# Encoder layer with an S5 mixer: the start of the S5 stage, the order of its loop and its hand-over to the output projection rearranged

## The reference

```python
lam_dt  = (lam_re + i*lam_im) * exp(log_step)
b_bar   = (exp(lam_dt) - 1) / lam * b
h[t]    = exp(lam_dt) * h[t-1] + b_bar @ u[t]            # one direction; the other runs over flipped tokens
y       = gelu(y_fw + y_bw + d * u)
out     = (y * sigmoid(y @ w_glu + b_glu)) @ w_out
h       = layer_norm(ALPHA * x + out)
```

## Time and profile before

| what | value |
|---|---|
| median of 3 runs | 2645.22 us |
| the profiled execution's own time | 2644.07 us |
| its span, first to last instruction | 2642.3 us |
| mean granted TensorE clock | 0.973 |
| PE busy / DVE busy / POOL busy over the span | 94% / 73% / 28% |

### The profile page before, as it was taken

How to read it: one execution, slowest core, us unless ns; L and a number is a source line. 1 busy time by engine, 2 the same in 40 slices (tenths; PEclk the granted TensorE clock), 3 DMA queues, 4 the chain that set the end, 5 groups by cost and what they waited for, 6 DMA issues and landing times. The chain is left out here.

```text
span 2642.3 us, 39850 instructions
## 1 busy us (share of the span) xinstructions
PE 2488.7 (94%) x12860; PEld 2085.5 (79%) x12860; DVE 1920.4 (73%) x3122; ACT 900.0 (34%) x1455; POOL 727.2 (28%) x557
## 2 busy tenths in 40 slices
PE   7678799999999999999999999998799999999997
PEld 6567687878888878887888888887677888887886
DVE  8879826777877758884667666676586777785887
ACT  3223324243333335523322223223124333333641
POOL 6768810243333310001111111112024333331000
PEclk9888899999999999999999999999899999999999
DMA  4143314056677678722010110100404667667863
GB/s 146 56 118 105 97 56 160 13 150 214 192 222 214 204 264 281 233 102 63 25 41 24 40 32 24 40 24 16 159 8 135 203 207 220 209 200 259 296 207 130
DMA packets 442288, 355.97 MB, mean 135 GB/s; under 512 B 30272, under 2 KB 376512, under 8 KB 438464
## 3 DMA queue, kind: packets, MB, share of 16 engines
q1 hardware_dynamic: 442176, 354.52, 42.9%
HBM read 296.31 MB, written 58.13 MB: 134 GB/s over the span
## 5 line engine op out<-in xcount | busy, mean ns | idle before, releaser
L2514 PE MATMUL ps<-aT_hi,w_hi 128*128 128x512 f32 x624 | 250.7, 402 | 3.8 <-DVE hg_q_raw L2793 2.0
L2464 POOL TENSOR_TENSOR w_lo<-w_raw_plain,w_hi 128x1024 fp32r<-128x1024 f32 x38 | 90.9, 2401 | 575.3 <-ACT w_hi L62 575.3
L2514 PE MATMUL ps<-aT_hi,w_lo 128*128 128x512 f32 x624 | 245.2, 393 | 0.0
L2514 PE MATMUL ps<-aT_lo,w_hi 128*128 128x512 f32 x624 | 243.8, 391 | 0.0
L616 PE MATMUL ps<-aT_hi,hgo_w_sets 128*128 128x512 f32 x640 | 203.0, 393 | 0.0
L616 PE MATMUL ps<-aT_hi,s5o_w_sets 128*128 128x512 f32 x640 | 202.7, 393 | 0.0
L1284 POOL TENSOR_TENSOR s5o_w_sets_plain<-s5o_w_sets_plain 128x512 f32<-128x512 f32 x80 | 109.9, 1374 | 216.7 <-DMA s5o_w_sets_plain<-in_ffn_w_in_dram 216.7
L1284 POOL TENSOR_TENSOR hgo_w_sets_plain<-hgo_w_sets_plain 128x512 f32<-128x512 f32 x80 | 110.6, 1383 | 212.8 <-DMA hgo_w_sets_plain<-in_ffn_w_in_dram 212.8
L616 PEld LDWEIGHTS ps<-aT_hi,hgo_w_sets 128*128 128x128 f32 x640 | 120.4, 188 | 26.4
L616 PEld LDWEIGHTS ps<-aT_hi,s5o_w_sets 128*128 128x128 f32 x640 | 120.2, 188 | 26.3
L2514 PEld LDWEIGHTS ps<-aT_hi,w_hi 128*128 128x128 f32 x624 | 117.5, 188 | 26.9 <-DVE hg_q_raw L2793 2.4
(11 more groups left out here) (445 smaller groups left out, 6246.9 us busy)
## 6 DMA issues: line engine op xcount, KB each, us to landing
s5o_w_sets_plain<-in_ffn_w_in_dram SPq DMA_DIRECT2D x168, 256.0 KB, 3.2
hgo_w_sets_plain<-in_ffn_w_in_dram SPq DMA_DIRECT2D x168, 256.0 KB, 3.3
w_raw_plain<-in_hg_w_in_dram SPq DMA_DIRECT2D x40, 512.0 KB, 3.9
aT_hi_plain<-in_ffn_w_out_dram SPq DMA_DIRECT2D x64, 256.0 KB, 4.6
s5o_w_sets_plain<-in_ffn_w_in_dram SPq DMA_DIRECT2D x96, 128.0 KB, 2.7
hgo_w_sets_plain<-in_ffn_w_in_dram SPq DMA_DIRECT2D x96, 128.0 KB, 2.8
s5o_hidden<-s5o_home_plain SPq DMA_DIRECT2D x11, 1024.0 KB, 7.0
hgo_hidden<-hgo_home_plain SPq DMA_DIRECT2D x11, 1024.0 KB, 6.8
```

The lines of the kernel that those rows point to most:

```text
L2464: g.tensor_tensor(w_lo[b][:, :, :], w_raw[b][:, :, :], w_hi[b][:, :, :].bitcast(F32), ALU.subtract).then_inc(E[f"w_lo_done{b}"], 1)
L2514: ins = t.matmul(ps[:, half, :], w[b][:, kk, :], x[:, kk, cols], start=(kk == 0 and q == 0), stop=(kk == KT - 1 and q == 2))
```

## The change

- **Front.** The tables on DVE shrink to `tables_to_inverse`; eight operations go to POOL (`first_power`). DVE makes both halves of `bl(0)`; POOL waits until the scan factors (`mu`) are done before it splits w_in slice 1 and makes `bl(1)`. `cl(0)` forward moves from POOL to DVE, behind `scan(0)`, and from POOL's front goes one `make_cl`. `inputs(2)` is cut in two, around `start_state(1)`; on ACT `place_c(0)`, a half of `keep_u(2)` and `keep_state(0)` come ahead of `place_c(1)`.
- **Loop.** For n = 2 to 5 the first half of `inputs(n+2)` stays ahead of `turn_bl(n+1)` and the second half goes behind it. On ACT the second `keep_u(n+2)` and `split_w(n+3)` go behind `place_b`, `keep_min`, `place_c`. `turned_diagonal(n)` moves to just after the first level of `scan(n)`. POOL's and SP's order in the loop stay.
- **Hand-over.** Inside the S5 block ACT and DVE split the first piece of w_out ahead of the gates of slice 6 and the first four rows of x ahead of those of slice 7; PE's last gate slice runs row by row over both halves. The next block's PE starts on these without a wait. Some buffers are laid out anew for that (`UNDER_FIRST_WEIGHTS`, `s5_gap`, `k.first` and `k.hi0` allocated in the S5 block).

The core of the diff, in the order of the file (the next block first, then the S5 block by SP, PE, ACT, DVE, POOL):

```diff
-        k.first, k.hi0, k.lo0 = (k.sb("w_" + n, [P, PIECE], F32R, keep=True) for n in ("raw0", "hi0", "lo0"))
+        k.lo0 = k.sb("w_lo0", [P, PIECE], F32R, keep=True)
...
-            s.wait_ge(S["w_lo"], KT)
+            s.wait_ge(S["w_lo"], KT - PIECE_DONE)
             load_rows(gamma_mid, beta_mid)
-            s.wait_ge(S["x_lo"], KT)
+            s.wait_ge(S["x_lo"], KT - ROWS_DONE)
             for half in range(2):
                 tiles = slice(4 * half, 4 * half + 4)
                 s.dma_start(h[:, tiles, :], residual_v[:, tiles, :]).then_inc(S[f"back{half}"], 16)
-            s.wait_ge(S["w_lo"], 2 * KT)
+            s.wait_ge(S["w_lo"], 2 * KT - PIECE_DONE)
...
-                        t.wait_ge(S["x_lo"], at + 1)
-                        t.wait_ge(S["w_lo"], 4 * n + at + 1)
+                        if at >= ROWS_DONE:
+                            t.wait_ge(S["x_lo"], at + 1 - ROWS_DONE)
+                        if n or not PIECE_DONE:
+                            t.wait_ge(S["w_lo"], 4 * n + at + 1 - PIECE_DONE)
                         for tt in range(4):
                             project(n, at, tt, 2 * tt + dh)
                 else:
-                    t.wait_ge(S["x_lo"], KT)
-                    t.wait_ge(S["w_lo"], 4 * n + 4)
+                    t.wait_ge(S["x_lo"], KT - ROWS_DONE)
+                    t.wait_ge(S["w_lo"], 4 * n + 4 - PIECE_DONE)
...
-                    if not natural or n and at == 3:
+                    if (4 * n + at == KT - 1) if natural else (4 * n + at >= ROWS_DONE):
                         split_x(4 * n + at)
-                    if n or not natural:
+                    if n:
...
-                    split_x(4 * n + at)
-                    split_piece(n, at)
+                    if 4 * n + at >= ROWS_DONE:
+                        split_x(4 * n + at)
+                    if n or not PIECE_DONE:
+                        split_piece(n, at)
...
+            s.wait_ge(S["next_lo"], FIRST_ROWS + 4)
...
-                    t.wait_ge(S["bl"], (n + 1) * BL - BL // 2)
+                    t.wait_ge(S["bl"], (n + 1) * BL)
                 if n == 0:
                     t.wait_ge(S["c_kept"], 8)
                 elif n == 1:
                     t.wait_ge(S["min_kept"], 4)
                 else:
                     t.wait_ge(S["kern_rows_done"], n)
-                    t.wait_ge(S["cl_fw"], (n - 1) * CLF)
+                    t.wait_ge(S["cl_fw"], n * CLF)
                 for m in range(4):
                     if n == 0:
-                        t.wait_ge(S["bl" if m < 2 else "bl_bw"], BL // 4 * (m % 2 + 1))
+                        t.wait_ge(S["bl"], BL // 4 * (m + 1))
...
-                t.wait_ge(S["cl"], (n + 2) * CLS)
-                t.wait_ge(S["cl_fw"], (n or 1) * CLF if n < KT - 1 else (n - 1) * CLF + CLS)
+                t.wait_ge(S["cl"], (n + 1) * CLS)
+                t.wait_ge(S["cl_fw"], ((n or 1) + 1) * CLF if n < KT - 1 else n * CLF + CLS)
...
             turn_bl(1)
-            inputs(2, (0, 1))
+            inputs(2, (0,))
             start_state(1)
+            inputs(2, (1,))
             make_kern(0)
...
                 across_chunks(n - 1)
                 if 2 <= n < KT - 2:
-                    inputs(n + 2, (0, 1))
+                    inputs(n + 2, (0,))
                 if n < KT - 1:
                     turn_bl(n + 1)
+                if 2 <= n < KT - 2:
+                    inputs(n + 2, (1,))
 
...
                     if kks[-1] == KT - 1:
                         ins.then_inc(S["unit"], 1)
+                    elif n == KT - 1 and half == 1:
+                        ins.then_inc(S["row_free"], 1)
...
                 t.wait_ge(S[f"glu_lo{n % 2}"], n // 2 + 1)
-                for half in range(2):
-                    t.wait_ge(S["gated"], 2 * (n - 4) + half + 1)
-                    gate_part(n, (half,), range(KT))
+                if n < KT - 1:
+                    for half in range(2):
+                        t.wait_ge(S["gated"], 2 * (n - 4) + half + 1)
+                        gate_part(n, (half,), range(KT))
+                else:
+                    t.wait_ge(S["gated"], 2 * (n - 4) + 2)
+                    for kk in range(KT):
+                        gate_part(n, (0, 1), (kk,))
...
-                a.wait_ge(S["min_kept"], 4 * (n + 1))
+                a.wait_ge(S["min_kept"], 4 * ((n or 1) + 1))
+                if n == 1:
+                    a.wait_ge(S["cl_fw"], CLF)
...
             keep_min(1)
+            place_c(0)
+            keep_u(2, (0,))
+            keep_state(0)
             place_c(1)
-            keep_u(2)
+            keep_u(2, (1,))
             split_w(3)
-            keep_state(0)
             keep_kern_rows(0)
             place_b(1)
             for n in range(1, KT):
                 keep_kern_rows(n)
                 if n >= 2:
                     keep_y(n - 1)
-                if n + 2 < KT:
+                if n == 1:
                     keep_u(n + 2)
-                if n + 3 < KT:
                     split_w(n + 3)
+                if n >= 2 and n + 2 < KT:
+                    keep_u(n + 2, (0,))
                 if n == KT - 2:
                     split_glu(0)
                 if n + 1 < KT:
...
                         place_c(n + 1)
                 if n == 1:
                     keep_y(0)
+                if n >= 2 and n + 2 < KT:
+                    keep_u(n + 2, (1,))
+                    if n + 3 < KT:
+                        split_w(n + 3)
...
             for n in range(KT):
+                if n == KT - 2:
+                    a.wait_ge(S["early"], 16)
+                    a.wait_ge(S["out_done"], KT)
+                    for at in range(4):
+                        split_hi(a, in_four(k.first)[:, at, :], in_four(k.early)[:, at, :]).then_inc(S["next_w_hi"], 1)
+                if n == KT - 1:
+                    for kk in range(FIRST_ROWS):
+                        a.wait_ge(S["row_free"], kk + 1)
+                        a.wait_ge(S["mixed"], 2 * (kk + 1))
+                        split_hi(a, in_tokens(k.aT_hi[:, kk, :]), in_chunks(row(kk))).then_inc(S["next_x_hi"], 1)
                 gates(n)
...
-            def tables_to_first_power():
-                v.wait_ge(S["tab_act"], 4)
-                done(v.tensor_tensor(W["c1"], W["half"], W["half"], ALU.mult))
-                done(v.tensor_scalar(W["c1"], W["c1"], -2.0, None, ALU.mult))
-                done(v.tensor_scalar(W["cos"], W["c1"], 1.0, None, ALU.add))
+            def tables_to_inverse():
+                v.wait_ge(S["tab_act"], 2)
                 done(v.tensor_scalar(W["t"], W["tanh"], -1.0, 1.0, ALU.mult, ALU.add))
                 done(v.reciprocal(W["t"], W["t"]))
-                done(v.scalar_tensor_tensor(W["em"], W["tanh"], 2.0, W["t"], ALU.mult, ALU.mult))
-                done(v.tensor_scalar(W["e"], W["em"], 1.0, None, ALU.add))
                 done(v.memset(asc[:, 0, :, 0], 1.0))
                 done(v.memset(asc[:, 1, :, 0], 0.0))
-                done(v.tensor_tensor(asc[:, 0, :, 1], W["e"], W["cos"], ALU.mult))
-                done(v.tensor_tensor(asc[:, 1, :, 1], W["e"], W["sin"], ALU.mult))
-                assert link.n == FIRST_POWER
+                assert link.n == INVERSE
 
             def tables_to_input_factors():
+                v.wait_ge(S["exp"], EXP)
...
-                if n == KT - 1:
+                if n == 1:
+                    turned_diagonal(0)
+                if n >= 2:
                     turned_diagonal(n)
                 for lv in range(1, LV):
                     last = whole(lv, False, last)
-                if n == 1:
-                    turned_diagonal(0)
-                if 2 <= n < KT - 1:
-                    turned_diagonal(n)
...
-            tables_to_first_power()
+            tables_to_inverse()
             for n in range(4, XT):
                 split_x(n)
             tables_to_input_factors()
             v.wait_ge(S["b_kept"], 4)
             make_b_bar(v, 0)
             v.wait_ge(S["pow"], POW)
-            make_bl(v, 0, (0,))
+            make_bl(v, 0)
             scan_factors()
             v.wait_ge(S["c_turned"], 4)
             v.memset(state[:, :, :, 0], 0.0).then_inc(S["pads"], 1)
             scan(0)
+            v.wait_ge(S["c_placed"], 1)
+            make_cl_in_psum(v, 0)
             for n in range(1, KT):
                 if n < KT - 1:
-                    v.wait_ge(S["c_placed"], n)
+                    v.wait_ge(S["c_placed"], n + 1)
...
             for n in range(KT):
+                if n == KT - 2:
+                    for at in range(4):
+                        v.wait_ge(S["next_w_hi"], at + 1)
+                        v.tensor_tensor(in_four(k.hi0)[:, at, :], in_four(k.early)[:, at, :],
+                                        in_four(k.first)[:, at, :].bitcast(F32), ALU.subtract).then_inc(S["next_lo"], 1)
+                if n == KT - 1:
+                    for kk in range(FIRST_ROWS):
```

(48 more changed lines are left out.)

36 lines of the change are left out of this document (24 added, 12 removed).

## The result

Over the runs of both kernels the changed one took 2652.3 us (median of 8), the kernel before 2644.8 (median of 8): ratio 1.0026, 95% interval 1.0015 to 1.0037. That is 7.5 us slower, on the side and near the size of the forecast (2653.8). The profiled execution of the changed kernel took 2650.0 us, its span 2648.2 us, at a mean granted clock of 0.974.

The account below looks back on a forecast made before the run. PE was taken as the bound over the span, with a loop through ACT's and POOL's splits pacing the S5 stage. Terms -0.4 + 11.3 - 2.3 = plus 8.6 us gave 2652.7 profiled, 2653.8 as median; range 2641 to 2667.

Parts of the forecast that it names:

- front: Start of the S5 stage up to the end of `inputs(4)`: forecast at 165.1 us against 165.52, minus 0.4 us.
- loop: Two periods from `inputs(4)` to `inputs(6)`, forecast at 37.1 us each against 31.67 and 31.22: plus 11.3 us.
- hand-over: Passage from S5 to the next block: PE forecast to start at 411.0 instead of 413.25, minus 2.3 us.
- the border: The hand-over to the next block, forecast at minus 2.3 us, bounds minus 5.3 to nothing.
- the turns between the halves: 16 turns put ahead of the input product's second half: 3.0 us taken, between 2.2 and 3.69.
- DVE's stall at the diagonal: In the loop `turned_diagonal(n)` waits for kernel rows that need POOL's `make_cl`: 6 us, costed at nothing.
- the scan factors: 26 short DVE operations in the front, forecast at 5.5 us instead of 23.0, ending at 46.7.
- all steps from there to the end of `inputs(4)` are the same: Front, from step 2's turns, forecast 3.4 us sooner: nothing changes but the turns now in the middle, 3.0 us.
- DVE sets the pace: Faster rival: with w_in's split in time, the loop is DVE's 30.2 us and the time 2634; chance 0.12.
- the zero: The end of `inputs(n+2)`, from which the forecast counts times in a loop period.
- The forecast's chain for the kernel before: Loop: end of `inputs(n+2)`, ACT's copy and split, POOL's split, `make_cl`, PE's kernel, output products, next `inputs`; 31.67 and 31.22 us.
- The clock rival: Slower rival: the product's second half runs at half pace, 4.6 us in each of two periods: 2663; chance 0.13.

Follow-up runs that it names:

- the old order: Changed kernel with both halves of the input product ahead of the turns again: 0.9983 of the kernel before; with the border undone too: 0.9993.
- the diagonal's experiment: Changed kernel with DVE's turned diagonal back at its old place behind the scan's upward levels: 1.0028 of the kernel before.
- moving POOL's split: Changed kernel with POOL's split of the weights behind the six instructions of `make_cl` in the loop: 0.9943 of the kernel before.

## Why the prediction was right, step by step

The forecast's sum was -0.4 (front), +11.3 (loop), -2.3 (hand-over). The three parts by themselves, as differences of ratios times 2644.8: the loop 1.0026 - 0.9983 = 0.0043, plus 11.4 us; the border 1.0026 - 1.0039 = -0.0013, minus 3.4 us (by the old order, 0.9983 - 0.9993, minus 2.6); the front 0.9993 - 1, minus 1.9 us, with nothing inside its interval. Each of them has an interval of 3 to 4 us around it, so by the times only the loop's sign is shown; the border's rests on PE's wait in the traces, and the front's is open. The experiments also cut the change in another way than the forecast: the 3.0 us of the turns inside `inputs(4)`, which the forecast has in its front, belong to the loop order. By that cut it forecast -3.4 for the front, +14.3 for the order and -2.3 for the border.

In the traces, cut as the forecast is, the front came at +2.4, the loop at +10.2 and the hand-over at -3.4, in all 9.2 at the next block's first product. That the sum is so near 8.6 owes something to luck: the front was forecast 2.8 us too low, the other two 1.1 too high each, and a scatter of several us lies behind them.

**Loop: right in mechanism and nearly in size.** The period was forecast at 37.1 us and came at 36.6; PE's waits were named at 2.4 us ahead of the turns (0.4 to 1.3 came) and about 5 ahead of the kernel (4.1 to 5.8 came). The term that was off is the turns between the halves, 3.0 us: the halves came 196.42 to 198.72 apart, 2.3, near the lower bound of 2.2. DVE's stall at the diagonal was put at 6 us and took 2.3 to 4.5, as the scan's first level took 5.4 us (172.21 to 177.57) where 3 were charged, and costing it at nothing is what the diagonal's experiment bears out.

**Front: right at the scan factors, wrong behind them.** 5.5 us for the factors was exact, the x split gained 2.1 and not 3.1 us, `bl(0)` started 1.0 us later than forecast, and that 1.0 and 0.2 more stand at the third turns (123.72, forecast 122.5). The step that failed is "all steps from there to the end of `inputs(4)` are the same". The turns themselves were not the same (stretch, length, busy and count of PE, PEld, DVE, ACT, POOL, granted clock; the changed kernel, then the kernel before):

```profile
123.70:127.60 3.90, 3.83 (x16) 3.06 (x16) 0.00 (x0) 1.80 (x4) 3.85 (x3) 0.50 0.00 0
```

```profile
125.80:129.70 3.90, 2.30 (x20) 1.69 (x16) 0.25 (x1) 2.79 (x6) 3.59 (x3) 1.00 0.09 22
```

Behind a wait of 4.75 us for POOL they ran at a granted clock of 0.50; in the kernel before they followed other products without a wait and ran at 1.00. ACT's `keep_y(0)` behind them began 4.72 us behind the first turn instead of 3.43: 1.3 us that the forecast charged at nothing. From there the chain goes through ACT (changed kernel):

```profile
128.44 1.07 ACT L1955 ACTIVATE h<-ps 128x512 f32<-128x512 f32 x2
...
138.03 1.06 ACT L1961 ACTIVATE h<-h 128x1024 f32<-128x1024 f32 x1 [5.28 <-DMA h<-s_scratch_y]
139.00 0.25 ACT L1935 ACTIVATE s_kern_rows<-ps 128x112 f32<-128x112 f32 x1
```

y goes through DRAM and back, and ACT's copy of the kernel rows stands behind it in ACT's queue. So `inputs(4)` began at 153.49, 0.8 us sooner than before and not 3.4, and the turns between its halves added 3.2. The state products, which took 6.26 us where they had taken 3.71, cost nothing here: PE had the kernel ready at 137.41, before ACT came to it, and from the state products' start to the output products it was 13.92 us, against 13.70 in the kernel before.

**Hand-over: right in mechanism, a little small.** PE's wait was forecast near 4 and came at 3.14 us; the four rows were done at 420.97 (412.07 + 8.90), 2.2 us each as against the 2.45 that was charged.

**The rivals.** "DVE sets the pace" didn't come; "it decides if `bl` is ready less than 26 us behind the zero" is what moving POOL's split does, and then the gain is 15 us where the rival named 11 (its own terms, -6.7, -3.6 and -2.3, make 12.6). But it isn't DVE that sets the period then: it is PE's own round, 24.7 us plus the state products with the halved order and 25.0 to 25.1 with the old one, and where the state products take only 3.71 us it is POOL's ring of 28.9 us. The forecast's chain for the kernel before, through POOL's split and `make_cl`, was thus only one of two about equally long rounds, and the shorter one: with state products of 6.65 us PE didn't wait for `cl` there, and where those products took 4.98 us the chain came at 31.08 us.

The clock rival came in part. The second half of the product behind the turns ran at the full level (1.00, 2.4 GHz, 198.80 to 204.40), so its price of 9 us didn't come. That the loop's bursts pay for the throttle in every pass, as the Trainium skill has it (TensorE: Matmul & The Clock Gate, "HAM oscillation — how this bites in real kernels"), is borne out in two places. One is the state products, in the kernel before just as much. The other is new: behind the wait of 4.1 to 5.8 us for `cl` the products of the kernel and those within the chunks ran near the lower level (changed kernel, then the kernel before):

```profile
216.19:220.80 4.61, 4.61 (x48) 4.21 (x48) 2.91 (x6) 0.42 (x2) 4.27 (x8) 0.63 0.02 4
```

```profile
177.85:180.80 2.95, 2.95 (x50) 2.67 (x48) 2.78 (x6) 0.42 (x2) 2.64 (x6) 1.00 0.03 6
```

These 1.6 us a round cost no time, since PE then waited for POOL's `bl` all the same; they are a part of why it waited 0.4 to 1.3 us there and not 2.4.

## What to carry to other kernels

When one queue serves two consumers, put behind each other first what is ready and what is urgent, last what still waits for another engine: a POOL instruction of 2.35 us ahead of 7.7 us of ready work made a ring 6.5 us longer. Before reordering a fast engine's work around a result, follow the new late piece through every queue back to that result. And undo the parts of a compound change one at a time: here a loss of 11 us hid a gain of 3, and the kernel went from 7 us slower to 15 us faster than before once one line on another engine moved.

## What the hardware showed

**The clock behind equal waits.** The state products of step 2 start behind the same wait of 2.58 us on the same step in all kernels. In the kernel with both halves behind the turns and in the changed one:

```profile
130.00:133.70 3.70, 3.69 (x64) 3.44 (x64) 3.53 (x9) 2.58 (x4) 3.54 (x4) 1.00 0.44 167
```

```profile
130.20:136.40 6.20, 6.20 (x68) 6.03 (x72) 5.49 (x12) 2.54 (x4) 5.81 (x9) 0.58 0.46 150
```

A granted clock of 1.00 (2.4 GHz) in one, 0.58 in the other, so for most of that stretch the lower level of 1.2 GHz, though the code up to there is the same in both. In the loop it varies likewise between 3.71 and 6.65 us behind waits of 1.60 to 2.21 us. The idle just ahead doesn't decide it; what does, these runs don't show. For readers of traces this means that two kernels with periods 1 to 2 us apart need their state products compared before an order is called better.

**A short DVE operation waits for a whole POOL operation.** Besides the copies above, the first short operation of the changed kernel's front, 13.89 us, took 2.30 us and ended as POOL's first split did. In the kernel before three of four of the factors' steps took 1.1 to 1.2 us beside POOL's of 1.06, and 0.22 alone in the changed kernel. The Trainium skill (SBUF — State Buffer, "Who interferes with whom") says that copies and tensor-scalar operations in a two-port mode, and operations with two inputs in SBUF, take an interface that DVE shares with POOL, and that the later one stands until the other's instruction is over. The rows agree: the durations are those of POOL's instructions, not of DVE's. What POOL did beside the factors cost DVE 17.5 us there, and a POOL split moved under DVE work is not free.
